# Decode samples with their states as fixed operands and one query column each, and other places for steps around the passages of an FP32 decoder layer

## What is computed

```python
def retention_block(q, k, v, s_prev, log_gamma):
    """S_n = gamma * S_{n-1} + k_n^T v_n ;  o_n = q_n S_n."""
    ...

def layer(h, pos, conv_prev, ret_prev, norm_mix, w_in, conv_w, w_out,
          norm_mlp, w_up, w_down, ret_fn):
    hn = rmsnorm(h, norm_mix)
    z = hn @ w_in
    u_in, c_gate, b_gate, q, k, v, g = jnp.split(z, SPLITS, axis=-1)
    ...
    o, ret_state = ret_fn(q, k, v, ret_prev.astype(q.dtype))
    y_ret = head_rmsnorm(o).reshape(Bsz, T, RET_WIDTH) * jax.nn.silu(g)
    h = h + jnp.concatenate([y_conv, y_ret], axis=-1) @ w_out
    hn2 = rmsnorm(h, norm_mlp)
    h = h + jnp.square(jax.nn.relu(hn2 @ w_up)) @ w_down
    return h, conv_state, ret_state
```

## Time and profile before

| | |
|---|---|
| median of 3 runs | 1164.9 us (1163.75 to 1165.01) |
| profiled execution, its own time | 1164.33 us |
| its span, first to last instruction | 1162.5 us |
| PE busy | 1143.7 us, 98% of the span |
| DVE, POOL, ACT busy | 764.1, 554.9, 432.9 us |
| TensorE clock granted, mean | 0.996 of full |

### The profile page before, as it was taken

The page is one execution under the profiler, slowest core; times in us unless marked ns, Lnnn a source line. Parts: engine busy times, 40 slices in busy tenths (PEclk is TensorE's granted clock), DMA queues, the critical chain, the costliest instruction groups (busy, mean ns, idle before and its releaser), DMA issues.

```text
span 1162.5 us, 22545 instructions
## 1 busy us (share of the span) xinstructions
PE 1143.7 (98%) x8689; PEld 1119.7 (96%) x8689; DVE 764.1 (66%) x1143; ACT 432.9 (37%) x859; POOL 554.9 (48%) x541
## 2 busy tenths in 40 slices
PE   9999999999999999998999999999999999999996
PEld 7899999999999999998999999999999999999996
DVE  4345446456355675787777777777877767777756
ACT  6423313214124433543333333334544444544414
POOL 0154243253150330143233242322989999998992
PEclk9999999999999999999999999999999999999999
DMA  6431211211301232253534435346864544454213
GB/s 203 133 111 37 76 54 54 74 54 40 88 19 58 58 108 92 72 167 109 183 119 147 146 124 178 110 145 230 280 204 129 183 153 143 136 187 136 87 38 146
DMA packets 153992, 139.79 MB, mean 120 GB/s; under 512 B 6794, under 2 KB 118131, under 8 KB 153901
## 3 DMA queue, kind: packets, MB, share of 16 engines
q1 hardware_dynamic: 148799, 135.50, 36.4%
q10 hardware_dynamic: 5102, 3.05, 0.9%
HBM read 98.07 MB, written 40.47 MB: 119 GB/s over the span
## 4 chain that ended last, share of the span: by engine, by line
PE 83%; POOL 10%; DVE 3%; issue 1%; DMA 1%; ACT 1%; SPq 0%; POOLq 0%; ACTq 0%; DVEq 0%
PE pair L1867 14%; PE pair L1868 14%; PE pair L1869 14%; PE pair L1668 8%; PE pair L1670 8%; PE pair L1669 8%; POOL dn_lo L772 7%; PE pair L1844 3%; PE pair L1846 3%; PE pair L1845 3%; PE pair L1710 1%; PE pair L1711 1%; PE pair L1713 1%; POOL dn_s L762 1%; POOL dn_s L760 1%
## 5 line engine op out<-in xcount | busy, mean ns | idle before, releaser
L1867 PE MATMUL pair<-m_hi,dn_hi 128*128 128x258 f32 (+2 forms) x896 | 255.6, 285 | 3.6 <-DVE a L1639 2.3
L1867 PE MATMUL pair<-b_hi,up_hi 128*128 128x258 f32 x896 | 255.7, 285 | 3.0 <-DVE hid L1515 3.0
L1868 PE MATMUL pair<-b_lo,up_hi 128*128 128x258 f32 x896 | 254.3, 284 | 0.0
L1868 PE MATMUL pair<-m_lo,dn_hi 128*128 128x258 f32 (+2 forms) x896 | 253.6, 283 | 0.0
L1869 PE MATMUL pair<-m_hi,dn_lo 128*128 128x258 f32 (+2 forms) x896 | 253.4, 283 | 0.0
L1869 PE MATMUL pair<-b_hi,up_lo 128*128 128x258 f32 x896 | 252.9, 282 | 0.0
L1668 PE MATMUL pair<-x_hi,w_both 128*128 128x344 f32 (+2 forms) x576 | 188.6, 328 | 0.0
L1670 PE MATMUL pair<-x_hi,w_both 128*128 128x344 f32 (+2 forms) x576 | 184.3, 320 | 0.0
L1669 PE MATMUL pair<-x_lo,w_both 128*128 128x344 f32 (+2 forms) x576 | 184.2, 320 | 0.0
L1639 DVE TENSOR_TENSOR hid<-pair,hid 128x516 f32<-128x516 f32 (+2 forms) x194 | 124.6, 642 | 77.3 <-PE pair L1869 75.7
L1867 PEld LDWEIGHTS pair<-b_hi,up_hi 128*128 128x128 f32 x896 | 169.9, 190 | 5.2 <-DVE up_lo L1431 3.2
(11 more groups left out here) (209 smaller groups left out, 2147.6 us busy)
## 6 DMA issues: line engine op xcount, KB each, us to landing
m_raw<-m_dram SPq DMA_DIRECT2D x56, 516.0 KB, 4.8
m_dram<-hid SPq DMA_DIRECT2D x64, 258.0 KB, 2.6
up_raw<-w_up_dram SPq DMA_DIRECT2D x32, 512.0 KB, 5.1
dn_raw<-w_down_dram SPq DMA_DIRECT2D x128, 128.0 KB, 2.4
w_raw<-w_in_dram SPq DMA_DIRECT2D x28, 512.0 KB, 3.7
m_dram<-hid SPq DMA_DIRECT2D x16, 774.0 KB, 3.9
h_dram<-hid SPq DMA_DIRECT2D x8, 516.0 KB, 3.3
h_in<-h_dram SPq DMA_DIRECT2D x16, 258.0 KB, 4.3
```

The source lines that it names most:

```text
L1867: m_.matmul(to, shs[k], mhs[k], start=STARTS[i] and k == 0, stop=False, skip_group_check=more)
L1868: m_.matmul(to, shs[k], mls[k], start=False, stop=False, skip_group_check=more)
```

## The change

Five things are changed.

1. **Samples.** The 8 matmuls at j = 12 now have the state (128 x 128) as the fixed operand and the sample's one query column, taken straight from `q_rot`, moving. Each result is one column of `SMP_B`: features on the partitions, as everywhere else. ACT copies the 128 x 8 block and squares it (`sq_smp`); PE sums the squares over the partitions with one more matmul, `ones` times the 8 columns, behind group j = 13; ACT takes the square root of it at j = 13, between two gates; DVE at j = 15 makes the reciprocal, scales and multiplies with the gate, three instructions of 128 x 8. `q_smp`, its copy and memset, the sample's share of the norms at j = 12 and 13 and the transpose L1808 are gone.
2. **DVE in unit q = 2 of the up product:** the four sums of unit 1 stand at steps 1 and 2, as those of unit 0 do in unit 1.
3. **ACT at the passage to the down product:** `mid_split(6)` stands behind the copy of the first result.
4. **SP:** the loads of `h_in` for the first unit stand ahead of the last two stores of the up product; in block 1 the loads of the stored results stand ahead of the weight loads of the same unit.
5. **DVE at the end:** of row group 4 only the reciprocal stands between the last steps; the scaling, whole, comes behind the last step.

```diff
-           (NW + 2, 2): (3, 0), (NW + 2, 3): (3, 1), (NW + 2, 5): (4, 0), (NW + 2, 6): (4, 1)}
+           (NW + 2, 2): (3, 0), (NW + 2, 3): (3, 1), (NW + 2, 5): (4, 2)}
...
-            store_row(LASTU, 6)
-            store_row(LASTU, 2)
             for n in range(KT):
                 sp.wait_ge(h_saved[n], 16)
             for i in range(4):
                 load_h(0, i)
+            store_row(LASTU, 6)
+            store_row(LASTU, 2)
             load_mid(7)
             load_mid(8)
+            def load_mids(wi):
+
+                b, n = wi // 4, wi % 4
+                if b < BLOCKS - 1:
+                    for j in ((2,), (3, 4), (5, 6), ())[n] if b == 0 else ((0, 1, 2), (3, 4), (5, 6), ())[n]:
+                        load_mid(7 * (b + 1) + j)
+
             for wi in range(NW):
                 b, n = wi // 4, wi % 4
+                if b == 1:
+                    load_mids(wi)
                 if wi + 2 < NW:
                     sp.wait_ge(dn_ready, 7 * wi + 7)
                     load_down(wi + 2)
...
-                if b < BLOCKS - 1:
-                    for j in ((2,), (3, 4), (5, 6), ())[n] if b == 0 else ((0, 1, 2), (3, 4), (5, 6), ())[n]:
-                        load_mid(7 * (b + 1) + j)
+                if b != 1:
+                    load_mids(wi)
...
-                        if j == 6:
-
-                            act.wait_ge(rot_added, 6 * h + 6)
-                            act.wait_ge(qsmp_set, 1)
-                            s.activation(q_smp[:, :, :].rearrange("p a b -> p (a b)")[:, 0:SAMPLES * SAMPLES:SAMPLES + 1],
-                                         q_rot[:, PROMPT:COLS], ACT.Copy).then_inc(qsmp_ready, 1)
...
-                            act.wait_ge(smp_done, h + 1)
-                            s.activation(o_smp[0:SAMPLES, :], SMP_B[0:SAMPLES, 0:P], ACT.Copy)
-                            s.activation(SMP_B[0:SAMPLES, P:2 * P], SMP_B[0:SAMPLES, 0:P], ACT.Square, accum_out=ms_o[0:SAMPLES, XT:XT + 1]).then_inc(smp_read, 1)
-                            act.wait_ge(smp_read, h + 1)
+                            act.wait_ge(smp_done, 2 * h + 1)
+                            s.activation(o_smp[:, :], SMP_B[:, 0:SAMPLES], ACT.Copy)
+                            s.activation(sq_smp[:, :], SMP_B[:, 0:SAMPLES], ACT.Square).then_inc(smp_read, 1)
...
+                        if j == 13:
+                            act.wait_ge(smp_done, 2 * h + 2)
+                            s.activation(std_smp[:, :], SMP_B[:, SAMPLES:2 * SAMPLES], ACT.Sqrt, scale=1.0 / DK, bias=eps).then_inc(smp_read, 1)
...
-                        for j in ((), (0,), (1,), (2,), (3,), (4, 5), (6,))[i]:
+                        for j in ((), (0,), (1,), (2,), (3,), (4, 5), ())[i]:
                             mid_split(j)
...
+                    if q == 0 and i == 0:
+                        mid_split(6)
...
                         if j == 15:
...
+                            dve.wait_ge(smp_read, 2 * h + 2)
+                            mine(d.reciprocal(r_smp[:, :], std_smp[:, :]))
+                            mine(d.tensor_tensor(o_smp[:, :], o_smp[:, :], r_smp[:, :], ALU.mult))
                             dve.wait_ge(silu_done, 3 * h + 3)
+                            ys = y_raw[:, bass.ds(4 + h, 1), PROMPT:COLS]
+                            d.tensor_tensor(ys, o_smp[:, :].unsqueeze(1), ys, ALU.mult)
...
-                    if i == 0 and q > 1:
+                    if i == 0 and q > 2:
                         for j in range(4):
                             mid_sum(q - 1, j)
...
-                    if q == 1 and i in (1, 2):
-                        mid_sum(0, 2 * i - 2)
-                        mid_sum(0, 2 * i - 1)
+                    if q in (1, 2) and i in (1, 2):
+                        mid_sum(q - 1, 2 * i - 2)
+                        mid_sum(q - 1, 2 * i - 1)
...
             first_sums()
+            final_norm(REST, 3)
             for i in range(FIRST_LATE, len(FINAL)):
                 final_norm(i)
...
                             pe.wait_ge(state_new, h + 1)
-                            pe.wait_ge(qsmp_ready, h + 1)
+                            pe.wait_ge(rot_added, 6 * h + 6)
                             for b in range(SAMPLES):
-                                ins = m_.matmul(SMP_B[0:SAMPLES, 0:P], q_smp[:, b, :], state[:, b, :], start=b == 0, stop=b == SAMPLES - 1)
+                                ins = m_.matmul(SMP_B[:, b:b + 1], state[:, b, :], q_rot[:, PROMPT + b:PROMPT + b + 1], start=True, stop=True)
                             ins.then_inc(smp_done, 1)
+                        if j == 13:
+                            pe.wait_ge(smp_read, 2 * h + 1)
+                            m_.matmul(SMP_B[:, SAMPLES:2 * SAMPLES], ones[:, :], sq_smp[:, :], start=True, stop=True).then_inc(smp_done, 1)
...
-                            m_.transpose(S_B[:, TAIL:TAIL + SAMPLES], o_smp[0:SAMPLES, :], ident[0:SAMPLES, 0:SAMPLES]).then_inc(yT_done, 1)
```

More of the change, by code:

```diff
@@ L660, in _ @@
             pool.wait_ge(main_read, G_IN)
-            g.memset(q_rot[:, 0:META], 0.0)
-            g.memset(q_smp[:, :, :], 0.0).then_inc(qsmp_set, 1)
+            g.memset(q_rot[:, 0:META], 0.0).then_inc(qrot_set, 1)
             def head(h, last):
@@ L1575, in final_norm @@
                 rows, j = final_rows(i), i % 2
-                if part != 1:
+                if part in (None, 0, 2):
                     dve.wait_ge(fstd_done, i + 1)
@@ L1584, in final_norm @@
                         dve.wait_ge(y_stored[i % 4], 16 * Y_FREE[i])
-                if part is None:
+                if part in (None, 3):
                     d.scalar_tensor_tensor(out=y_out[i % 4][0:rows, :].rearrange("p (h c) -> p h c", h=2), in0=final_bank(i)[0:rows, :, :],
@@ L1588, in final_norm @@
                                            op0=ALU.mult, op1=ALU.mult).then_inc(f_ready, 1)
-                else:
+                elif part < 2:
                     f0, f1 = CH * part, CH * part + CH
@@ L1815, in _ @@
             pe.wait_ge(ctail_done, HEADS)
-            pe.wait_ge(smp_read, HEADS)
+            pe.wait_ge(smp_read, 2 * HEADS)
             for h in range(HEADS):
```

20 lines of the change are left out of this document (8 added, 12 removed).

## The result

| | before | changed |
|---|---|---|
| median of 6 runs each | 1164.35 us (1163.57 to 1165.16) | 1157.32 us (1156.96 to 1158.97) |
| ratio, 95% interval | | 0.9941 (0.9929 to 0.9954) |
| profiled execution, its own time | 1164.33 us | 1157.55 us |
| its span | 1162.5 us | 1155.8 us |
| PE busy | 1143.7 us, 98% | 1142.2 us, 99% |

A forecast was written before the change was run, and what follows sets the result against it. PE, busy nearly the whole span, was taken as the bound; -4.0 - 1.3 - 2.7 - 0.5 + 2.2 = -6.3 us gave 1158.0 us for the profiled execution and a median of 1158.6 us, range 1154.5 to 1163.5.

The forecast's parts named there:

- case A: Whole kernel: the forecast itself, 1158.6 us, own range 1156 to 1161; chance 0.58.
- Unit 2: Up product, DVE: the 3.0 us wait and its low clock go, 0.7 us waits at step 5; -4.0 us.
- The passage: Up to down product: waits for ACT's copy and h_in go, DVE then bound; -1.3 us, from -0.5 to -1.8.
- rival C: Passages give half back as each removed wait moves the next one up; -8.5 becomes -4.3, 1162.8 us; chance 0.14.
- Block 1: Down product, SyncE: earlier m_raw loads remove PE waits of 1.0 and 1.3 us; -2.7 us, from -1.2 to -2.7.
- POOL's lead: Down product, near 953: POOL's lead over PE grows by 2.1 us, more than the 1.3 missing.
- The end: DVE: without L1591 ahead of the last L1639 the last transposes start sooner; -0.5 us, from 0 to -0.6.
- The samples: PE, four heads: new sample products cost +0.56 us a head, +2.2 us in all; from -1.7 to +6.6.
- p: Heads: time of one sample record with 128-column weights and one moving column, taken as 0.13 us.
- B: Heads: cheap loads, records at the transposes' 0.075 us, -1.7 instead of +2.2; 1154.7 us; chance 0.12.
- E: Heads: loads and one-column matmuls don't overlap, 0.39 us a record, 21 us in all; 1177.6 us; chance 0.10.
- D: Heads: the clock falls around the new block, 1.7 us a head, +6.8 us; 1165.4 us; chance 0.06.

The follow-up runs named there:

- order_only: The kernel before with the four changes of order and without the sample part; ratio 0.9933, -7.8 us against the kernel before.
- smp_wide: The changed kernel with all eight query columns moving past each state, ACT reading the eight wanted results; 1157.07 us in one execution.
- pass_only: The kernel before with only ACT's m_hi behind the copy and SP's h_in loads ahead of two stores; ratio 0.9996, -0.5 us.
- smp_twice: The changed kernel with the eight state products issued twice in a row; ratio 1.0061, +7.1 us against the kernel before.
- smp_k64: The changed kernel with only the upper 64 rows of each state and query column in the product; 1161.59 us in one execution.
- smp_only: The changed kernel with the four changes of order undone, so the sample part alone; ratio 0.9999, -0.1 us against the kernel before.
- mids_first: The changed kernel with the loads of stored results ahead of the h_in loads in block 0; 1157.52 us, ratio 0.9936 against the kernel before.
- residuals: mids_first plus, on DVE, unit 2's second pair of sums one step later and the passage's third m_lo behind the first h_in read; 1156.24 us.
- residuals_hi: residuals with ACT splitting the next block's first stored result one step sooner in blocks 1 to 6; 1155.75 us, ratio 0.9920.

## Where the prediction was right and where not

*The time* (1158.6, own range 1156 to 1161, measured 1157.3) was right, as case A. It is partly right by luck: the samples were put 2.3 us too dear, and the gain of the orders, 8.5, was put 0.7 us too large by `order_only` (7.8) and 1.2 by the pair of traces (7.26). The two errors have opposite signs and cancel in part. The parts timed alone add up: 0.1, 4.3, 1.4 and 0.5 us, with the end's 0.3 from the traces 6.6 of the 7.0.

*Unit 2* (-4.0, measured -4.06 in the traces, -4.3 alone): right, step by step, with the residual wait for u3 (0.7 forecast, 0.49 and 0.15 of restart). What the working didn't see is that its 1.7 us for the clock were one draw: 0.25 to 2.9 in four profiles.

*The passage* (-1.3): the step itself was right in mechanism and nearly in size, -1.09. The weakness of the term is what it left out: it stopped at step 3 of the first unit. A PE that comes earlier can meet late loads at the end of block 0, which is rival C's mechanism. Alone the edit was worth only 0.5 us (from a gain of 1.6 to a loss of 0.6), and in its trace that place took back 1.2. In the changed kernel the place took 0.5, but kernels with the old passage lose as much there, so that this 0.5 comes from the passage isn't shown.

*Block 1* (-2.7): the mechanism was right (loads earlier, the waits for `a` shrink), the size was not: -1.4 alone. The -2.3 of the pair of traces is nearer only because it takes in the 1.17 us at 871. The term counted both waits of one profile as if each stood in every execution. The 1.0 us at 871 stood in one of the four profiles without the edit, the one in which SP was slow to issue the weights; of the 1.3 near 953, 0.4 to 0.6 came back in most profiles, there or a block later. The argument on POOL's lead (2.1 us more, 1.3 missing) was too generous by that much.

*The end* (-0.5, measured -0.3): it has no run of its own, but the last transposes gain 0.27 to 0.31 us in each of the nine profiles with this edit and 0.01 in those without. L1591 went away as forecast, and L1645 then waited for PE's last product. The step forgot that the awaited read can't start before what it reads.

*The samples* (+2.2, measured -0.3 in the traces, -0.1 alone): the step that failed is p. The prediction had a load's 107 ns right from the rows and then added 22 ns for the moving, from the transposes' row; 0.106 leaves no room for them, and `smp_wide` shows that eight columns add nothing either. With 0.106 the forecast's own formula gives +0.13 a head. The rest is in the edges: entering the new block costs 0.16 between starts where it was 0.24; the `ones` product costs 0.22 in all, not two records and 0.19; the missing transpose is worth 0.05, not 0.13. Together -0.25 + 0.22 - 0.05 = -0.08 a head, the 0.3 us of the traces. The sentence on the Trainium skill's rule that spoke against this part (+0.6 us) was nearer than my price from a transpose.

*Rivals.* B (0.075 a record) and E (no overlap) are excluded by 0.106. C is shown for block 3, where a third to a half of the wait came back, and for the passage by `pass_only`'s trace alone; its size, half of all the gain, was too large. D didn't happen: the clock stays at 1.00 in the heads of the changed kernel. But what spoke against D were waits, that is, stretches in which PE idles; `smp_twice` and `smp_k64` show the clock fall with PE busy throughout, so they didn't bear on it.

## What to carry to other kernels

A wait read from one profile is a draw: before its size goes into a sum, ask what it would be if PE came half a us earlier or a load half a us later, and count waits with one root once. Where an edit takes a wait away at a passage, follow the same queues to the end of the next block, since the next load in line is often as late. And a run of matmuls with full weights and few moving columns cost 0.106 us a record here, whether one column moved or eight; keep it short, since the clock can fall in it or behind it, and that costs about as much as the run itself.

## What the runs showed of the hardware

- The granted clock fell to 0.50 with PE never idle: in or right behind a block of 32 records with one moving column in three of four heads, and behind one of 16 records with 64 rows in two of four. It stayed low for 3.4 to 6.8 us each time. Behind 16 records with 128 rows it stayed at 1.00 in every head of seven profiles (the changed kernel twice, `smp_only`, `smp_wide`, `mids_first`, `residuals`, `residuals_hi`).
- The same wait of 3.0 us, in the same place of the same program, was followed by the lower level for 3.4 us, for 6.8, or not at all (PEclk 0.89, 0.77 and 1.00 from 530 to 545 us). The kernel before spreads from 1162 to 1167 us, and the changed one, without this wait, from 1156.5 to 1159. The clock has a part in that spread: of the 47 executions of the kernel before timed beside the experiments, the 10 with a mean granted clock of 0.998 took 1161.9 to 1164.0 us, and the 5 with 0.995 or less 1164.7 to 1167.3.
- A record of a matmul with 128 fixed columns costs 0.106 us with one moving column and 0.107 with eight; with 64 rows in place of 128, 0.117.
- The same four weight loads took SP 1.91 us to issue in two profiles, 2.69 and 3.17 in two others, and the load that stood behind them came later by as much.
